# A gate chunk ahead of the attention, selection rounds beside it, and four smaller reorderings in a two-layer decoder trunk

## The chip, the cores and the metric

The kernel runs on one core of a Trainium2 chip. The metric is device time in microseconds of that core, the median of three runs. PE is the matmul engine (its weight loads are PEld), DVE the vector engine, ACT the scalar engine, POOL the GpSimd engine, and SP the engine whose queue issues the weight transfers.

## What is computed

Two layers on 256 tokens of width 1024, all in float32. Each layer mixes tokens by two causal attentions fed by one projection, gates both by sigmoids of that projection, and projects once more; then comes a dense SwiGLU (layer 0) or a top-2-of-8 expert SwiGLU (layer 1), each sub-layer followed by a residual and a LayerNorm.

```python
c_q, c_kv, k_r, dq, dk, dv, iq, ik, iw, gates = split_cols(x @ w_in)
y_a = mla_branch(c_q, c_kv, k_r, pos, ...) @ w_o_mla       # dense causal, 8 heads
y_b = dsa_branch(dq, dk, dv, iq, ik, iw, pos) @ w_o_dsa     # causal, top 64 keys of a query, 8 heads
g = sigmoid(gates); merged = g[..., :D] * y_a + g[..., D:] * y_b
h = merged @ w_out
x = layer_norm(ALPHA * x + h)
f = swiglu(x) if layer 0 else sum over 8 experts of comb[:, e] * swiglu_e(x)
x = layer_norm(ALPHA * x + f)
```

## The kernel before

Each engine has its own program, an order written out by hand, and semaphores between them. All large products are float32 by splitting: a weight unit of 128 x 2048 values (1 MB) lands in one of seven slots (`raw`), ACT casts it to its leading part (`make_head`, `job_head`), DVE subtracts that to get the rest (`make_rest`, `job_rest`), both into one of three slots (`split`), and PE then makes three matmuls for every block of 128 rows (`product`, lines 1528 to 1530): rest of the activations by head of the weights, head by head, head by rest. A head waits until PE has used the unit three before; a rest waits for its head; PE waits for the rest. SP refills a slot of `raw` when its rest is made.

A layer's mixer (`pe_mixer`) projects nine chunks of 512 columns (the last 456), each of two units and two token tiles. Chunks 0 to 4 hold what the attentions need (units 0 to 9). Units 10 to 12 are the latent projections, units 13 and 14 are chunk 5, units 15 to 20 are chunks 6, 7 and 8, all gate columns. Units 21 to 28 are the branch and output projections.

On the first layer PE turns the first half of x (`turn_half`), makes unit 0 for token tile 0, turns the second half of x, makes unit 0 for tile 1, and goes on to unit 1, which needs the second half. ACT and DVE copy every turned half into its head and rest (`cast_x`, `rest_x`).

The attention runs over 16 units (8 heads of the dense kind, then 8 of the sparse kind), software-pipelined on PE: in step i come `qk(i)`, one gate piece, `turn_probs(i - 2)`, in steps 2 to 9 a second gate piece, and `pv(i - 3)`. A gate piece is six matmuls; chunks 6 to 8 have 24. `qk(u)` waits for the row maxima of unit u - 2. DVE makes the maxima (`maxima(u)`); beside them stand the rests of units 17 to 22, five of eight selection rounds (`best_keys`; two max and two replace operations each), `selection`, and `norm_heads(0)`, which waits for `pv(7)` and which `pv(8)` waits for. Two rounds stand ahead of the attention and one much earlier. ACT makes the exponentials (`exps`), copies turned probabilities (`turned_probs`), evacuates gate chunks (`chunk_tile`) and casts heads 17 to 23.

The experts run as eight jobs of 42 units each (`all_jobs`, `JOB`; w1 and w3 in two halves for each of seven hidden groups g, then w2). Of the first job: before its fourth unit DVE has a block of small operations on one partition and on the expert weights, from the wait for `pos_mm` to `routed` (lines 1048 to 1066). In the middle of the job, ACT casts all of x (line 747) and DVE subtracts (line 1131), for the gather of experts 1 and 2 (`gather_pair`), which PE starts at the last w3 of the job. At its end DVE scales x into y (line 1140). POOL makes the picks of the pair (`pair_picks`, line 575) once the expert weights are there.

Of the kernel before, what the change touches and what calls it, by code (L numbers as in the profile page):

```python
# [18 lines left out]
ALU = mybir.AluOpType  # L19
# [6 lines left out]
P = 128  # L26
# [126 lines left out]
def build(nc, a, out):  # L153
    ctx = ExitStack()
    with ctx:
# [328 lines left out]

        def by_slot(b):

            return b[:, :].rearrange("p (k s) -> p k s", k=2)
# [211 lines left out]
        def act_experts(act):  # L699
# [9 lines left out]
            def job(j, kind):  # L709
# [19 lines left out]
                for m, (w, g, half) in enumerate(JOB):  # L729
# [15 lines left out]
                    if kind == "first" and (w, g, half) == ("w2", 2, 0):  # L745
                        act.wait_ge(rests_made, EARLY[0] + 1)
                        act.copy(x_parts[HEAD][:, :, :], x[:, :, :]).then_inc(x_head_made, 1)
# [16 lines left out]
        def _(act):  # L764
# [25 lines left out]
            for l in range(DEPTH):  # L790
# [94 lines left out]
                chunk_tile(ATT, 1)  # L885

# [16 lines left out]
                for i in range(16 + 1):  # L903
# [4 lines left out]
                    if i == 0:  # L908
                        head(17)
                    if i == 2:  # L910
                        head(18)
                    if i in (3, 4):
                        chunk_tile(6, i - 3)
                    if i == 5:
                        head(19)
                    if i == 6:
                        head(20)
                    if i in (7, 8):
                        chunk_tile(7, i - 7)
                    if i == 9:  # L920
                        head(21)
                    if i == 11:
                        head(22)
# [81 lines left out]
        def dve_experts(dve, step):  # L1005
# [42 lines left out]
            E = EXPERTS  # L1048
            dve.wait_ge(pos_mm, 2)
            over, s1, s2, s4 = (flags[0:1, i * 16:(i + 1) * 16] for i in range(4))  # L1050
            step(dve.tensor_scalar(over[:, E:2 * E], bank[4][0:1, 0:E], float(CAP), None, ALU.is_gt))

            dve.wait_ge(exp_done, 1)
            step(dve.tensor_tensor(r_exp, r_exp, r_sel, ALU.mult))
            step(dve.reduce_sum(r_one[:, :, 1:2], r_exp, AX_X))
            step(dve.reciprocal(r_one[:, :, 2:3], r_one[:, :, 1:2]))
            dve.tensor_tensor(r_comb, r_exp, r_one[:, :, 2:3].to_broadcast([P, T, EXPERTS]), ALU.mult).then_inc(placed, 1)
            dve.wait_ge(placed, 1)
            dve.tensor_copy(cur[:, 2:4], r_comb[:, :, 0:1].rearrange("p t n -> p (t n)")).then_inc(comb_put, 1)

            for src, dst, by in ((over, s1, 1), (s1, s2, 2), (s2, s4, 4)):
                step(dve.tensor_tensor(dst[:, E:2 * E], src[:, E:2 * E], src[:, E - by:2 * E - by], ALU.add))
            step(dve.tensor_copy(jobs[0:1, 0:E], over[:, E:2 * E]))
            step(dve.tensor_tensor(jobs[0:1, E:2 * E], s4[:, E:2 * E], over[:, E:2 * E], ALU.subtract))
            step(dve.tensor_copy(jobs[0:1, 2 * E:2 * E + 1], s4[:, 2 * E - 1:2 * E]))
            dve.sem_inc(routed, 1)
# [22 lines left out]
            def job(j, kind):  # L1089
# [28 lines left out]
                for m, (w, g, half) in enumerate(JOB):  # L1118
# [10 lines left out]
                    if kind == "first" and (w, g, half) == ("w2", 2, 1):  # L1129
                        dve.wait_ge(x_head_made, 1)  # L1130
                        dve.tensor_tensor(x_parts[REST][:, :, :], x[:, :, :], x_parts[HEAD][:, :, :].bitcast(F32), ALU.subtract).then_inc(x_rest_made, 1)
# [6 lines left out]
                if kind == "first":  # L1138
                    for t in range(T):
                        step(dve.tensor_scalar(y[:, t, :], x[:, t, :], ALPHA, None, ALU.mult))  # L1140
# [15 lines left out]
        def _(dve):  # L1156
# [133 lines left out]
            for l in range(DEPTH):  # L1290
# [123 lines left out]
                best_keys(range(1, 3))  # L1414
# [23 lines left out]
                for u in range(16):  # L1438
                    maxima(u)
                    if u == 0:  # L1440
                        rest(17)
                    if u < 5:
                        best_keys(range(3 + u, 4 + u))
# [608 lines left out]
```

## Time and profile before

| what | us |
|---|---|
| median of three runs | 1624.46 (1624.42 to 1627.68) |
| the profiled execution | 1625.77 |
| its span, first to last instruction | 1624.1 |
| PE busy | 1591.0 (98%) |
| DVE busy | 1293.2 (80%) |
| ACT busy | 1024.6 (63%) |

The span is what the profile's rows lie in; 1.7 us lie around it. Busy shares are averages over stages. A matmul's own duration is longer than its distance to the next, since they overlap: 512 columns are shown with 390 ns and follow each other every 228 ns. So a wait of PE is read from a gap or from a bracket behind a row, not from the busy share.

### The profile page before, as it was taken

What the parts mean: (1) busy time and instruction counts of PE and PEld (TensorE: products, weight loads), DVE (VectorE), ACT (ScalarE), POOL (GpSimd) and SP (SyncE); (2) the same over time, 40 slices, a digit from 0 to 9 for tenths busy, and PEclk for the clock granted to TensorE, in tenths of its full rate; (3) what the DMA queues carried; (4) which work ended last, traced back from release to release, by engine and by line L of the source; (5) the groups of instructions that cost most, each with busy time, mean ns of one, the idle gap of its engine ahead of it and who ended that gap; (6) DMA issues with size and microseconds to landing.
All of it is one profiled execution on the core that took longest, in us unless ns stands there. A gap on an engine that the chain in (4) does not pass through costs nothing.

```text
span 1624.1 us, 19196 instructions
## 1 busy us (share of the span) xinstructions
PE 1591.0 (98%) x7629; PEld 1322.8 (81%) x7630; DVE 1293.2 (80%) x1302; ACT 1024.6 (63%) x947; POOL 58.9 (4%) x54
## 2 busy tenths in 40 slices
PE   8999999999999999999999999999999999999996
PEld 7888788888788788878888888888888888888885
DVE  6794675445788468899889888889888889888887
ACT  5655544343465645776777776777776777776773
POOL 0000000000000002000000100000100000100000
PEclk9999999999999999999999999999999999999998
DMA  9543366556453355999999999999999999999992
GB/s 326 181 140 117 105 219 208 184 184 201 135 176 130 104 181 178 361 358 324 368 372 363 362 377 328 366 378 365 370 373 327 366 375 360 373 374 328 370 372 85
DMA packets 230687, 453.13 MB, mean 279 GB/s; under 512 B 9920, under 2 KB 15552, under 8 KB 230592
## 3 DMA queue, kind: packets, MB, share of 16 engines
q1 hardware_dynamic: 228400, 447.60, 78.1%
q10 hardware_dynamic: 2192, 4.23, 0.7%
q8 instruction: 63, 1.03, 0.3%
q14 instruction: 32, 0.26, 0.0%
HBM read 450.75 MB, written 1.05 MB: 278 GB/s over the span
## 4 chain that ended last, share of the span: by engine, by line
PE 90%; DVE 7%; ACT 2%; issue 1%; DMA 0%; DVEq 0%; ACTq 0%
PE bank L1528 27%; PE bank L1530 27%; PE bank L1529 27%; PE bank L2003 3%; DVE split L425 2%; PE bank L1698 1%; ACT split L419 1%; PE bank L1916 1%; DVE split L441 1%; PE bank L1889 0%; PE bank L1890 0%; PE bank L1727 0%; PE bank L1726 0%; ACT split L436 0%; DVE x L1241 0%
## 5 line engine op out<-in xcount | busy, mean ns | idle before, releaser
L441 DVE TENSOR_TENSOR split<-raw,split 128x2048 fp32r<-128x2048 f32 x327 | 747.7, 2289 | 103.1 <-ACT split L436 101.9
L436 ACT CAST split<-raw 128x2048 fp32r<-128x2048 f32 x327 | 625.5, 1914 | 185.5 <-PE bank L1530 185.5
L1528 PE MATMUL bank<-split,xe_pair 128*128 128x512 f32 x784 | 310.0, 395 | 0.5 <-DVE split L441 0.5
L1530 PE MATMUL bank<-split,xe_pair 128*128 128x512 f32 x784 | 305.9, 390 | 0.0
L1529 PE MATMUL bank<-split,xe_pair 128*128 128x512 f32 x784 | 305.3, 389 | 0.0
L425 DVE TENSOR_TENSOR split<-raw,split 128x2048 fp32r<-128x2048 f32 (+3 forms) x96 | 208.3, 2174 | 111.3 <-ACT split L419 110.9
L419 ACT CAST split<-raw 128x2048 fp32r<-128x2048 f32 (+3 forms) x96 | 174.4, 1817 | 168.6 <-PE bank L1530 168.3
L1528 PE MATMUL bank<-split,xT 128*128 128x512 f32 (+2 forms) x544 | 217.8, 400 | 4.3 <-DVE split L425 2.4
L1530 PE MATMUL bank<-split,xT 128*128 128x512 f32 (+2 forms) x544 | 208.7, 384 | 0.0
L1529 PE MATMUL bank<-split,xT 128*128 128x512 f32 (+2 forms) x544 | 208.7, 384 | 0.0
L1528 PE MATMUL bank<-split,hT 128*128 128x512 f32 x488 | 190.6, 391 | 0.0
L1530 PE MATMUL bank<-split,hT 128*128 128x512 f32 x488 | 190.0, 389 | 0.0
L1529 PE MATMUL bank<-split,hT 128*128 128x512 f32 x488 | 190.0, 389 | 0.0
L1530 PEld LDWEIGHTS bank<-split,xe_pair 128*128 128x128 f32 x784 | 147.2, 188 | 31.4
L1528 PEld LDWEIGHTS bank<-split,xe_pair 128*128 128x128 f32 x784 | 147.2, 188 | 29.8 <-issue 0.9
L1529 PEld LDWEIGHTS bank<-split,xe_pair 128*128 128x128 f32 x784 | 147.4, 188 | 29.3
L1528 PEld LDWEIGHTS bank<-split,xT 128*128 128x128 f32 x544 | 102.6, 189 | 30.6 <-issue 10.1
L1530 PEld LDWEIGHTS bank<-split,xT 128*128 128x128 f32 x544 | 102.7, 189 | 20.3
L1529 PEld LDWEIGHTS bank<-split,xT 128*128 128x128 f32 x544 | 102.9, 189 | 17.7
L1530 PEld LDWEIGHTS bank<-split,hT 128*128 128x128 f32 x488 | 91.6, 188 | 19.2
L1528 PEld LDWEIGHTS bank<-split,hT 128*128 128x128 f32 x488 | 91.7, 188 | 18.7 <-DVE hT L970 0.2
L1529 PEld LDWEIGHTS bank<-split,hT 128*128 128x128 f32 x488 | 91.6, 188 | 18.5
(248 smaller groups left out, 1604.1 us busy)
## 6 DMA issues: line engine op xcount, KB each, us to landing
raw<-moe_w_dram SPq DMA_DIRECT2D x330, 1024.0 KB, 6.1
raw<-w_in_dram SPq DMA_DIRECT2D x31, 1024.0 KB, 5.1
raw<-dense_w_dram SPq DMA_DIRECT2D x30, 1024.0 KB, 5.1
raw<-w_out_dram SPq DMA_DIRECT2D x8, 1024.0 KB, 5.1
early<-moe_w_dram SPq DMA_DIRECT2D x6, 1024.0 KB, 14.0
raw<-w_o_mla_dram SPq DMA_DIRECT2D x4, 1024.0 KB, 5.1
raw<-w_o_dsa_dram SPq DMA_DIRECT2D x4, 1024.0 KB, 5.4
raw<-w_in_dram SPq DMA_DIRECT2D x4, 912.0 KB, 5.2
```

The lines of the kernel that those rows point to most:

```text
L419: act.copy(split[:, n % SPLIT, HEAD, 0:k * cols], raw[:, n % RAW, 0:k * cols]).then_inc(heads_made, 1)
L425: dve.tensor_tensor(split[:, n % SPLIT, REST, 0:k * cols], raw[:, n % RAW, 0:k * cols], split[:, n % SPLIT, HEAD, 0:k * cols].bitcast(F32) ...
L436: act.copy(split[:, n % SPLIT, HEAD, :], landing(n, j)[:, :]).then_inc(heads_made, 1)
L441: dve.tensor_tensor(split[:, n % SPLIT, REST, :], landing(n, j)[:, :], split[:, n % SPLIT, HEAD, :].bitcast(F32), ALU.subtract).then_inc(r ...
L1528: pe.matmul(out_, act_[REST], w[HEAD], start=first, stop=False)
L1529: pe.matmul(out_, act_[HEAD], w[HEAD], start=False, stop=False)
L1530: return pe.matmul(out_, act_[HEAD], w[REST], start=False, stop=last)
L1698: ins = pe.matmul(bank[4 + u % 2][:, t * P:t * P + keys], q, kk, start=True, stop=True)
L1916: ins = pe.matmul(bank[PAIR_BANKS[r]][:, i * 2 * CAP:(i + 1) * 2 * CAP], x_parts[part][:, t, k * P:(k + 1) * P], pair_pick[:, t, :], start ...
L2003: return pe.transpose(dst, src, ident[:, :])
```

## The change

- On layer 0, PE turns the second half of x after the first two blocks of unit 0, tile 0, where before it did so after all four.
- All eight pieces of chunk 6 go ahead of the attention; in every one of the 16 steps there is one gate piece, of chunk 7 or 8. ACT casts heads 17 and 18 and evacuates chunk 6 ahead of its first exponentials, and the other heads and evacuations follow at new steps.
- On DVE three more selection rounds stand ahead of the attention (five instead of two), with rest 17 between them; rounds 6 and 7 follow in steps 1 and 3, `selection` in step 5, rests 18 to 22 after steps 2, 6, 9, 12 and 14.
- In the first expert job the block of small operations goes behind the rest that follows the fourth unit's `hidden(0)`. The cast and the subtraction of x become four pieces of 512 columns, in the w2 of groups 1 to 4. The scaling into y becomes four pieces beside w3 of groups 3 to 6.

```diff
@@ act, expert jobs
-                    if kind == "first" and (w, g, half) == ("w2", 2, 0):
+                    if kind == "first" and (w, half) == ("w2", 0) and 1 <= g <= 4:
+                        t, at = piece_of_x(g - 1)
                         act.wait_ge(rests_made, EARLY[0] + 1)
-                        act.copy(x_parts[HEAD][:, :, :], x[:, :, :]).then_inc(x_head_made, 1)
+                        act.copy(x_parts[HEAD][:, t, at], x[:, t, at]).then_inc(x_head_made, 1)
@@ act, ahead of and beside the attention
                 chunk_tile(ATT, 1)
+                head(17)
+                for t in range(T):
+                    chunk_tile(6, t)
+                head(18)
...
-                    if i == 0:
-                        head(17)
-                    if i == 2:
-                        head(18)
-                    if i in (3, 4):
-                        chunk_tile(6, i - 3)
-                    if i == 5:
+                    if i == 4:
                         head(19)
-                    if i == 6:
+                    if i in (6, 8):
+                        chunk_tile(7, (i - 6) // 2)
+                    if i == 8:
                         head(20)
-                    if i in (7, 8):
-                        chunk_tile(7, i - 7)
-                    if i == 9:
+                    if i == 10:
                         head(21)
-                    if i == 11:
+                    if i == 12:
                         head(22)
@@ dve, expert jobs
-            (wait for pos_mm, weights, crowding, routed: lines 1048 to 1066)
+            def weights_and_crowding(): (the same lines)
...
-                    if kind == "first" and (w, g, half) == ("w2", 2, 1):
-                        dve.wait_ge(x_head_made, 1)
-                        dve.tensor_tensor(x_parts[REST][:, :, :], x[:, :, :], ...)
+                    if kind == "first" and (w, g, half) == ("w3", 0, 1):
+                        weights_and_crowding()
+                    if kind == "first" and (w, half) == ("w2", 1) and 1 <= g <= 4:
+                        t, at = piece_of_x(g - 1)
+                        dve.wait_ge(x_head_made, g)
+                        dve.tensor_tensor(x_parts[REST][:, t, at], x[:, t, at], ...)
+                    if kind == "first" and (w, half) == ("w3", 0) and g >= NG - 4:
+                        t, at = piece_of_x(g - (NG - 4))
+                        step(dve.tensor_scalar(y[:, t, at], x[:, t, at], ALPHA, None, ALU.mult))
...
-                if kind == "first":
-                    for t in range(T):
-                        step(dve.tensor_scalar(y[:, t, :], x[:, t, :], ALPHA, None, ALU.mult))
@@ dve, ahead of and beside the attention
                 rest(16)
-                best_keys(range(1, 3))
+                best_keys(range(1, 4))
+                rest(17)
+                best_keys(range(4, 6))
...
-                    if u == 0:
-                        rest(17)
-                    if u < 5:
-                        best_keys(range(3 + u, 4 + u))
-                    if u == 4:
+                    if u == 2:
                         rest(18)
+                    if u in (1, 3):
+                        best_keys(range(6 + u // 2, 7 + u // 2))
+                    if u == 5:
+                        selection()
                     if u == 6:
-                        selection()
-                    if u == 7:
                         rest(19)
-                    if u == 8:
+                    if u == 9:
                         rest(20)
                     if u == 10:
                         norm_heads(0)
-                    if u == 11:
+                    if u == 12:
                         rest(21)
-                    if u == 13:
+                    if u == 14:
                         rest(22)
@@ pe_mixer
                     if (l, c, half) == (0, 0, 0) and i % 2 == 0:
+                        if (i, t) == (2, 0):
+                            pe.wait_ge(x_in2, 16)
+                            for tile in range(T):
+                                turn_half(0, tile, 1)
                         pe.wait_ge(rests_made if i else first_rest, 1)
...
+            for f in range(8):
+                gate_piece(f)
...
-            f = 0
+            f = 8
...
-                if 2 <= i < 10:
-                    gate_piece(f)
-                    f += 1
@@ gather_pair
-                    pe.wait_ge(x_rest_made, 1)
+                    pe.wait_ge(x_rest_made, 2 * T)
```

## Rows read from the trace of the kernel before

**Rows 1.** The page, section 1: busy time, share of the span, instructions.

```profile
PE 1591.0 (98%) x7629; PEld 1322.8 (81%) x7630; DVE 1293.2 (80%) x1302; ACT 1024.6 (63%) x947; POOL 58.9 (4%) x54
```

**Rows 2.** Who PE waited for: us in total, times, longest.

```profile
PE bank L1698 <- DVE mx L1428: 3.8, 2, 1.9
PE bank L1528 <- DVE split L441: 2.8, 3, 1.2
PE bank L1528 <- DVE split L425: 2.4, 2, 2.2
```

**Rows 3.** Timeline of the start: start, duration, engine, line, operation, idle before.

```profile
10.39 0.40 PE L1530 MATMUL bank<-split,xT 128*128 128x512 f32 x1
...
12.28 1.03 PE L2003 MATMUL bank<-ident,x 128*128 128x128 f32 x8
...
12.91 1.08 ACT L777 CAST xT<-bank 128x512 fp32r<-128x512 f32 x2 [3.74 <-PE bank L2003]
...
15.83 4.49 DVE L425 TENSOR_TENSOR split<-raw,split 128x2048 fp32r<-128x2048 f32 x2 [1.00 <-ACT split L419]
...
18.26 0.71 PE L1528 MATMUL bank<-split,xT 128*128 128x512 f32 x1 [2.18 <-DVE split L425]
```

**Rows 4.** The tile x in the first 20 us: second load's issue; times to landing.

```profile
L506 SPq DMA_DIRECT2D x<-x_dram x1: 470/470/470, 2.3 to 2.3; - x1
...
DMA to landing us min/median/max: 4.1/5.6/7.0
```

**Rows 5.** Stretches: PE, PEld, DVE, ACT, POOL busy; granted clock; DMA share, GB/s.

```profile
18.00:22.00 4.00, 3.74 (x10) 2.96 (x11) 3.83 (x11) 1.81 (x1) 0.00 (x0) 0.57 1.03 380
108.00:113.00 5.00, 3.10 (x15) 2.29 (x15) 4.80 (x22) 1.35 (x5) 0.00 (x0) 1.00 0.58 201
168.00:172.00 4.00, 4.00 (x12) 3.11 (x11) 3.45 (x4) 2.27 (x5) 0.00 (x0) 0.57 0.02 4
```

**Rows 6.** Timeline at the entry of the attention, layer 0.

```profile
104.58 1.89 ACT L419 CAST split<-raw 128x2048 fp32r<-128x2048 f32 x1
...
106.50 2.29 DVE L425 TENSOR_TENSOR split<-raw,split 128x2048 fp32r<-128x2048 f32 x1 [2.85 <-ACT split L419]
...
108.71 0.61 DVE L1343 MAX8 top<-score 128x8 f32<-128x128 f32 x2
...
110.14 0.29 DVE L1425 CUSTOM_DVE_ANT_0 sm<-bank,causal 128x128 f32<-128x128 f32 x1
...
111.04 0.92 PE L1698 MATMUL bank<-kTm,qTm 96*128 96x128 f32 x4 [1.90 <-DVE mx L1428]
```

**Rows 7.** Timeline: starts of qk(6), qk(7); of qk(10), qk(11).

```profile
124.35 0.87 PE L1698 MATMUL bank<-kTm,qTm 96*128 96x128 f32 x4
...
128.78 0.87 PE L1698 MATMUL bank<-kTm,qTm 96*128 96x128 f32 x4
...
142.54 0.92 PE L1698 MATMUL bank<-dT 64*128 64x128 f32 x4
...
145.78 0.92 PE L1698 MATMUL bank<-dT 64*128 64x128 f32 x4
```

**Rows 8.** Timeline of DVE: norm_heads(0) begins, and what follows it.

```profile
145.88 0.20 DVE L1434 RECIPROCAL rden<-den 128x8 f32<-128x8 f32 x1 [1.54 <-PE bank L1727]
...
147.56 0.28 DVE L1425 CUSTOM_DVE_ANT_0 sm<-bank,select 128x128 f32<-128x128 f32 x1
```

**Rows 9.** Timeline at the start of the first expert job.

```profile
637.56 0.15 DVE L1051 TENSOR_SCALAR flags<-bank 1x8 f32<-1x8 f32 x1
...
639.09 5.97 POOL L575 TENSOR_SCALAR pair_pick<-slot_no,small 128x128 fp32r<-128x128 f32 x3 [0.22 <-POOL small L570]
...
640.17 4.49 DVE L441 TENSOR_TENSOR split<-raw,split 128x2048 fp32r<-128x2048 f32 x2 [0.34 <-DVE jobs L1065]
...
642.52 0.50 PE L1528 MATMUL bank<-split,xeT 128*128 128x512 f32 x1 [1.23 <-DVE split L441]
```

**Rows 10.** Timeline: x into its rest, and the scaling into y.

```profile
701.36 2.29 DVE L1131 TENSOR_TENSOR x_rest_part<-x,x_head 128x2048 fp32r<-128x2048 f32 x1
...
754.57 1.41 DVE L1140 TENSOR_SCALAR y<-x 128x1024 f32<-128x1024 f32 x2
```

More of the change, by code:

```diff
@@ L483, in pair_half, with piece_of_x @@
             return slice(CAP, 2 * CAP) if kind == "even" else slice(0, CAP)
+        def piece_of_x(i):
+            return i // 2, slice(i % 2 * W, (i % 2 + 1) * W)
         def by_slot(b):
@@ L1046, in dve_experts @@
             make_rest(dve, FIRST + SPLIT - 1)
[L1048 to L1063, printed above, removed]
@@ L1064, in dve_experts, with weights_and_crowding @@
-            step(dve.tensor_tensor(jobs[0:1, E:2 * E], s4[:, E:2 * E], over[:, E:2 * E], ALU.subtract))
-            step(dve.tensor_copy(jobs[0:1, 2 * E:2 * E + 1], s4[:, 2 * E - 1:2 * E]))
-            dve.sem_inc(routed, 1)
+            def weights_and_crowding():
+                E = EXPERTS
+                dve.wait_ge(pos_mm, 2)
+                over, s1, s2, s4 = (flags[0:1, i * 16:(i + 1) * 16] for i in range(4))
+                step(dve.tensor_scalar(over[:, E:2 * E], bank[4][0:1, 0:E], float(CAP), None, ALU.is_gt))
+                dve.wait_ge(exp_done, 1)
+                step(dve.tensor_tensor(r_exp, r_exp, r_sel, ALU.mult))
+                step(dve.reduce_sum(r_one[:, :, 1:2], r_exp, AX_X))
+                step(dve.reciprocal(r_one[:, :, 2:3], r_one[:, :, 1:2]))
+                dve.tensor_tensor(r_comb, r_exp, r_one[:, :, 2:3].to_broadcast([P, T, EXPERTS]), ALU.mult).then_inc(placed, 1)
+                dve.wait_ge(placed, 1)
+                dve.tensor_copy(cur[:, 2:4], r_comb[:, :, 0:1].rearrange("p t n -> p (t n)")).then_inc(comb_put, 1)
+                for src, dst, by in ((over, s1, 1), (s1, s2, 2), (s2, s4, 4)):
+                    step(dve.tensor_tensor(dst[:, E:2 * E], src[:, E:2 * E], src[:, E - by:2 * E - by], ALU.add))
+                step(dve.tensor_copy(jobs[0:1, 0:E], over[:, E:2 * E]))
+                step(dve.tensor_tensor(jobs[0:1, E:2 * E], s4[:, E:2 * E], over[:, E:2 * E], ALU.subtract))
+                step(dve.tensor_copy(jobs[0:1, 2 * E:2 * E + 1], s4[:, 2 * E - 1:2 * E]))
+                dve.sem_inc(routed, 1)
@@ L1128, in job @@
                         turned(g - 1)
-                    if kind == "first" and (w, g, half) == ("w2", 2, 1):
-                        dve.wait_ge(x_head_made, 1)
-                        dve.tensor_tensor(x_parts[REST][:, :, :], x[:, :, :], x_parts[HEAD][:, :, :].bitcast(F32), ALU.subtract).then_inc(x_rest_made, 1)
+                    if kind == "first" and (w, g, half) == ("w3", 0, 1):
[3 more added lines that the diff above has]
+                        dve.wait_ge(x_head_made, g)
+                        dve.tensor_tensor(x_parts[REST][:, t, at], x[:, t, at], x_parts[HEAD][:, t, at].bitcast(F32), ALU.subtract).then_inc(x_rest_made, 1)
+                    if kind == "first" and (w, half) == ("w3", 0) and g >= NG - 4:
+                        t, at = piece_of_x(g - (NG - 4))
+                        step(dve.tensor_scalar(y[:, t, at], x[:, t, at], ALPHA, None, ALU.mult))
                     if kind in PAIR_GATHER and (w, g, half) == ("w3", NG - 1, 1):
@@ L1606, in pe_mixer @@
                     if (l, m) == (0, 0):
-                        keep_warm(pe, t, 0 if t else 4)
-                        pe.wait_ge(x_in2 if t else x_in, 16)
-                        for tile in range(T):
-                            turn_half(0, tile, t)
-                        keep_warm(pe, t, 0 if t else 4)
+                        if t == 0:
+                            keep_warm(pe, 0, 4)
+                            pe.wait_ge(x_in, 16)
+                            for tile in range(T):
+                                turn_half(0, tile, 0)
+                            keep_warm(pe, 0, 4)
                     if m == 0:
```

## Prediction

> **What bounds the kernel now.** First the busy shares: PE is busy for 98% of the span [rows 1]. Matmuls that merely follow one another cannot be made fewer by a reordering, and this change neither adds nor removes one. So all it can win is time in which PE stands still or runs slowly, and I read that directly: the table of who PE waited for. It has three lines that the change touches [rows 2]: the first qk that waits for a row maximum, 3.8 us in two times, one in each layer; rests of expert units, 2.8 us in three times; rests of mixer units, 2.4 us in two times, of which 2.2 us is one wait. That is 9.0 us out of 1624. The third view is the granted clock. After the 2.2 us wait at the start PE runs at 1.2 GHz for a while: the mean clock of 18 to 22 us is 0.57, so 4 x 0.43 = 1.7 us are lost there besides the wait. The same happens after the end of the attention, 168 to 172 us, and nothing of that kind after the wait at the entry of the attention, clock 1.00 in 108 to 113 us [rows 5]. Weight transfers are no bound in the rows of waits: no expert unit of PE, nor its head or rest, waits for a landing. If PE gets faster by some microseconds, the queues in front of it are filled by rests that are themselves released by PE, so they move with it.
>
> **The start (layer 0 only).** Before, PE turned the second half of x at 12.28, ACT began its casts at 12.91, and DVE could begin rest 1 at 15.83, after waiting 1.00 us for the head; PE went on at 18.26 [rows 3]. After, the turn comes behind six matmuls of unit 0 whose last begins at 10.39 and takes 0.23: at 10.62. The second half of x was issued at 2.3 and landed 7.0 us later, at 9.3 [rows 4], so the turn does not wait. The whole chain turn, cast, head 1, rest 1, PE moves by 12.28 - 10.62 = 1.66 us. It could be held up by the landing of unit 1, queued right behind x: if 1 MB takes the 2.7 us that a unit of PE lasts, it lands at 12.1, just ahead of the new time at which ACT is free (11.25 + 1.08 = 12.3). I take **1.6 us**, bounds 0.8 and 1.7. PE's own work of unit 0 is unchanged, it only ends 0.3 earlier, at 15.6, so the wait left is about 1.1 us instead of 2.2. On the clock: with 2.2 us of standing still it fell; after 1.9 us at 111.04 and 1.23 us at 642.52 it did not [rows 5, 6, 9]. 1.1 us is below both, so I take the drop as gone: **1.7 us**, bounds 0 and 1.7.
>
> The Trainium skill, page "TensorE: Matmul & The Clock Gate", section "What's actually happening", says that throttled is the default, that activity releases the throttle, and that the moment is run-variable because the monitor runs freely. By this rule a shorter stop is no promise: the drop could stay, or another stop could get one. The sum would then be 1.7 us smaller. The trace agrees with the variable part: a wait of 1.9 us had no drop, and a shorter one at the end of the attention had.
>
> **The attention, its entry (each layer).** Before: head 17 was cast at 104.58 (1.89), rest 17 followed at 106.50, a selection round took 108.71 to 110.14, and only then came the maxima of unit 1, for which PE stood until 111.04 [rows 6]. After, PE has chunk 6 first: 8 pieces x 6 matmuls x 0.228 = 10.9 us, so qk(0) comes at 112.1 instead of 101.2. Its units 15 and 16 are split already at that time (their rests end at about 100.0). DVE in the meantime: three rounds of 1.43, rest 17 of 2.21, two rounds [rows 6] = 9.4 us from 99.9, free at 109.3, ahead of qk(0). The first maxima are then made as soon as qk ends. On ACT head 18 stands behind the evacuation of chunk 6 at 112.1 and ends at about 114.6; a table load and the first exponentials end by about 117, turn_probs(0) is due at 118.2. So the wait of 1.9 us, with the restart 2.1 us from the last matmul, goes.
>
> **The attention, its steps.** A step with two pieces lasts 128.78 - 124.35 = 4.43 us, one with a single piece 145.78 - 142.54 = 3.24 us (456 columns, sparse unit) [rows 7]. Eight pieces leave the steps and eight are added ahead: PE's own work is conserved to within 0.1 us a piece, at nothing in my sum. What is lost is cover. Now every chain has to fit in 3.1 to 3.2 us a step from the first step on. I walked the three queues with the durations above. Maxima take 0.9 from their start [rows 6], a cast of a head 1.9, small ACT copies 0.5 each (1.08 for two [rows 3]), norm_heads 147.56 - 145.88 = 1.7 [rows 8]. The steps 10 to 15 have the same pieces as before, with the same two queues beside them, and had no PE wait, so the steady pitch holds. The one place where the new order is late is pv(8). Head 20 moves from step 6 to step 8. It now stands behind turned_probs(7) and an evacuation: turn_probs(7) begins at 139.1, then 0.5 + 0.4 + 0.5 + 1.8 = head done at 142.3. DVE has rest 20 queued in front of maxima(10) and norm_heads(0): 142.3 + 2.2 + 0.8 + 1.7 = 146.9. PE reaches pv(8) at 145.8 (two steps and 0.2 later). **PE waits about 0.9 us** (0.9 to 1.1 by the walk); bounds 0, if head 20 slips in earlier, and 2, if ACT is a copy later. Behind the waiting pv(8) on PE stands the rest of the attention, so this is paid in full. Net of the attention: 2.1 - 0.9 = 1.2 a layer, **2.4 us** for both. With no new wait 4.2, with 2.0 in each layer 0.2.
>
> **The small operations of the first job.** Before, they took DVE from 637.56 to 640.17, 2.6 us, right in front of rest 3, and PE waited 1.23 us (1.4 with the restart) for it at 642.52 [rows 9]. After, rest 3 begins when its head is done, 637.9, and PE goes on at 641.1. But the 2.6 us come back behind rest 6. A rest can't be far ahead, since its head waits for PE to use the unit three before: DVE ends rest 6 at about 648.2, then 2.6 us, then rest 7 of 2.2: 653.0. PE wants unit 7 at 641.1 + 4 x 2.72 + 0.4 (a turn) = 652.4. It waits 0.6, and 0.1 more for the next DVE step. **Gain 0.7 us**, bounds 0 and 1.4.
>
> These operations also release POOL's picks, whose first three took 5.97 us while two rests beside them took 4.49 [rows 9]. The Trainium skill, page "SBUF — State Buffer", section "Who interferes with whom", says that DVE and GpSimd share one pair of ports as an exclusive lock, and that the later one blocks fully. By that rule the picks would now fall on rests 7 to 9, which have no slack, and the 0.7 us could be gone; by the rows, two rests beside the picks lasted as long as two without them [rows 3], and the sum keeps it.
>
> **x in four pieces.** The subtraction of x, 2.29 us of DVE at 701.36 [rows 10], caused the second of the three expert waits, 1.06 us, with a follow-up of 0.1 to 0.2. A fourth of it is 0.6 us; DVE is idle 2.5 us of the 16.8 us of a group, and in w2 of each group a rest begins over 1 us ahead of its due time. ACT's pieces are 0.5 instead of 1.9. gather_pair now waits for four pieces, the last made in group 4, a whole group ahead. **Gain 1.2 us**, bounds 0.8 and 1.2.
>
> **y in four pieces.** 1.41 us of DVE at 754.57 [rows 10] made the third wait, the remaining 0.5 of the 2.8 [rows 2]. Pieces of 0.4 in groups 3 to 6, hidden by the same 2.5 us; groups 3 and 4 then have 1.0 us of both. **Gain 0.5 us**, bounds 0 and 0.6.
>
> **Sum.** 1.6 + 1.7 + 2.4 + 0.7 + 1.2 + 0.5 = 8.1 us. The profiled execution took 1625.77 (span 1624.1, the rest around it), so it would take 1617.7. The median of the runs is 1.3 us below the profiled one; I take the difference off the median: 1624.46 - 8.1 = **1616.4 us**.
>
> **The rivals.** (a) *The clock drop stays*, or moves to another stop: all waits go as said, 1.7 us less won, 1618.1. For it: the drop at the end of the attention follows shorter stops than the one now at the start. Against it: the stop is halved. (b) *The softmax chain is late in more places.* Each layer pays 1 to 2 us more, at the first turn_probs (1.2 us of slack in the walk), or in the expert job the 0.7 goes: 1618.5 to 1621. (c) *Better than said*: no wait at pv(8), or one clock drop at the end of an attention goes as well: 1613.0 to 1614.7. (d) *The change does not do what it says*: the time comes back at the next wait at each place, as at pv(8), 1624. (e) *Slower*: with one piece a step, the chain maxima, exponentials, copy sets the pitch, not PE, in the steps 0 to 9 where rounds and selection are added to it. Then these steps stay near the old 4.43 us while the 10.9 us of chunk 6 are paid ahead: 8 x 1.3 x 2 = 20.8 us lost, 8.1 + 1.7 won at most, about 1636. It decides against the change as soon as the steps of one layer lose 4.1 us to waits. Against it: steps 10 to 15 ran at 3.24 with up to 2.3 us of DVE and 1.9 us of ACT work added in a step, and a round is only 1.43.
>
> **Chances.** Forecast within 1.2 us: 0.50. (a) 0.20, (b) 0.12, (c) 0.08, (d) 0.05, (e) 0.05. The measurement can tell 0.2%, 3.2 us, from no change: faster means below 1621.2. Forecast, (a), (b) and (c) lie there: 0.90; (d) is the same, 0.05; (e) slower, 0.05. The range goes from the middle of (c), 1614.0, to the upper part of (b), 1620.2, and leaves out a little under 2 in 10.
>
> **What would show it.** Start: PE goes on to unit 1 at about 16.6, and 16 to 22 us have clock 1.00. Entry: no wait of L1698 for maxima; qk(0) near 108.8 (112.1 less the 3.3 won at the start). One new wait in each layer, pv(8) (L1725) for DVE's normed heads, near 0.9 us. First job: no wait at unit 3, one of about 0.6 at unit 7, none at x and y. Wrong would be: several waits for maxima or probabilities, a low clock at the start, or a rest in the first job late by more than 1 us.

## The result, and the profile after

| what | before | after |
|---|---|---|
| median | 1625.18 (4 runs, 1624.42 to 1627.68) | 1616.04 (4 runs, 1615.95 to 1618.1) |
| ratio | | 0.9944, 95% interval 0.9927 to 0.9961 |
| the profiled execution | 1625.77 | 1618.1 |
| its span | 1624.1 | 1616.3 |

9.1 us less (6.3 to 11.9 by the interval); forecast were 1616.4 and, as a sum, 8.1 us off a median of 1624.46, which with a fourth run is 1625.18. The changed kernel's profiled execution is the slowest of its four; the other three lie within 0.15 us of each other.

The changed kernel's page, section 1 (busy time, share, instructions) and the engines' shares of the chain that ended last:

```profile
PE 1589.0 (98%) x7629; PEld 1322.7 (82%) x7630; DVE 1293.8 (80%) x1307; ACT 1025.6 (63%) x950; POOL 57.0 (4%) x54
...
PE 95%; DVE 3%; ACT 1%; issue 1%; DMA 0%; DVEq 0%; ACTq 0%
```

The busy time is that of [rows 1] to within 2 us, with the same 7629 matmuls. What changed is who PE waited for, and there the answer to [rows 2] is (total us, times, longest):

```profile
PE bank L1739 <- ACT pT L910: 1.7, 2, 0.9
...
PE bank L1739 <- DVE proj L1444: 1.6, 2, 0.8
...
PE bank L1535 <- DVE split L425: 1.0, 2, 0.8
PE bank L1535 <- DVE split L441: 0.7, 1, 0.7
```

The line of the maxima (3.8 us) is gone. L441, the rests of expert units, went from 2.8 to 0.7 and from three waits to one; L425, the rests of mixer units, from 2.4 to 1.0. One line is new, L1444: pv(8) waits for the normed heads, 0.8 us in each layer. The first line was there before, with the same 1.7 us.

The early turn of x (first row) and the three places where PE now waits, from the timeline of PE, to be read beside [rows 3], [rows 8] and [rows 9]:

```profile
11.23 1.03 PE L2014 MATMUL bank<-ident,x 128*128 128x128 f32 x8
...
17.22 0.47 PE L1535 MATMUL bank<-split,xT 128*128 128x512 f32 x1 [0.82 <-DVE split L425]
...
144.30 0.41 PE L1739 MATMUL bank<-proj,pT 128*128 128x64 f32 x2 [0.81 <-DVE proj L1444]
...
648.42 0.50 PE L1535 MATMUL bank<-split,xeT 128*128 128x512 f32 x1 [0.67 <-DVE split L441]
```

The granted clock after the start stop, answering the first of [rows 5], and at the ends of the two attentions (busy time of PE, PEld, DVE, ACT, POOL; clock; DMA share; GB/s):

```profile
18.00:22.00 4.00, 4.00 (x19) 3.33 (x18) 3.72 (x12) 1.64 (x1) 0.00 (x0) 1.00 1.03 379
...
160.00:168.00 8.00, 6.17 (x28) 4.91 (x28) 5.09 (x7) 6.34 (x9) 0.00 (x0) 0.79 0.01 2
556.00:566.00 10.00, 8.17 (x50) 7.03 (x49) 4.87 (x7) 8.80 (x16) 0.00 (x0) 0.87 0.26 100
```

The low clock behind the start stop is gone (0.57 before); both ends of the attention still have theirs.

**Stretches.** To see where time went, every trace is divided at the same PE instructions, and the columns are the distances between their starts: the first product of unit 0 and the first product of unit 1; qk(0); the first branch matmul (oT); the first matmul on the dense hidden values (hT); the same for layer 1; the first unit of the first expert job; the first of the second job; the last PE instruction. The table is worked out from the timelines of PE. "Low" counts the places before the second job where eight or so large matmuls follow each other every 0.43 us instead of 0.228, that is at 1.2 instead of 2.4 GHz; a full one costs 1.5 to 1.7 us. A short one is one to four such matmuls at the very start. "Start overfill" is the first, mis-sized version of "start filled".

```
kernel     unit0-unit1  -qk(0)  -oT    -hT    -qk(0)  -oT    -job1  -job2   -end    low
before            9.12   82.90  66.56  89.11  244.23  66.56  65.22  125.61  853.48  3
after             8.05   92.19  54.39  89.12  255.15  54.38  65.23  123.35  853.17  2 + a short one
turn only         8.34   81.33  68.18  89.13  244.38  66.57  65.25  125.57  853.26  3 + a short one
attention only    9.13   93.81  54.37  87.57  255.27  54.39  63.69  125.61  853.32  1
experts only     10.82   82.91  66.52  89.11  244.27  66.56  65.22  123.34  853.20  4
start filled      9.05   81.35  68.18  89.11  244.26  66.59  65.22  125.61  853.39  3
start overfill   12.59   81.33  66.55  87.56  244.26  68.15  65.21  125.61  853.37  3
ends filled       7.44   92.22  54.33  87.60  255.26  54.34  63.71  123.31  853.22  0
head 20 early     7.45   92.20  53.32  89.06  255.14  53.32  63.68  123.34  853.22  1
rounds beside     7.79   92.20  54.37  89.10  255.26  54.38  65.21  123.35  853.27  2 + a short one
block alone       9.12   82.90  66.54  87.58  244.38  68.17  65.24  125.38  853.42  3
block in six      7.99   92.22  54.38  89.09  255.14  54.37  65.25  122.25  853.21  2 + a short one
three at once     7.43   92.22  53.28  88.63  255.12  53.28  63.70  122.26  853.25  1 shorter, in the LayerNorm
```

The same stretch has the same length in every kernel that has the same order in it, to within 0.15 us (0.3 in the long last one), or it differs by about 1.6 us: a low stretch that one execution has and another has not. So a part of the change is read by subtracting lengths, and the clock is read apart from it. What the table leaves out is the 12.1 us behind the last matmul. They are the same in every profile but that of the attention part alone, where they are 14.3, since DVE stood still there with nothing that it waited for; in the kernel before it waited 0.57 us at that place:

```profile
1611.84 0.21 DVE L1226 BATCH_NORM_AGGREGATE mv<-stat 128x2 f32<-128x12 f32 x1 [2.73 <-issue]
```

So not every difference between two executions is the clock's. For the executions without a trace there is the mean granted clock of each. It is 0.997 in the profile without a low stretch, 0.996 or 0.995 in those with one or two, and 0.994 or 0.993 in those with three or four: an estimate from these is 0.001 for each.

### The profile page after: what moved, and what is told of

It reads as the page before. It is cut to its first block, busy times and chain, and to the rows that moved or that the text cites. A ratio compares the mean times of both kernels' runs of the same rounds, so it can differ in the third digit from the quotient of the medians.

```text
span 1616.3 us, 19203 instructions
## 1 busy us (share of the span) xinstructions
PE 1589.0 (98%) x7629; PEld 1322.7 (82%) x7630; DVE 1293.8 (80%) x1307; ACT 1025.6 (63%) x950; POOL 57.0 (4%) x54
## 4 chain that ended last, share of the span: by engine, by line
PE 95%; DVE 3%; ACT 1%; issue 1%; DMA 0%; DVEq 0%; ACTq 0%
PE bank L1535 29%; PE bank L1537 29%; PE bank L1536 29%; PE bank L2014 4%; PE bank L1712 1%; PE bank L1927 1%; ACT split L419 1%; PE bank L1900 0%; PE bank L1901 0%; DVE split L441 0%; DVE x L1248 0%; PE bank L1741 0%; PE bank L1740 0%; PE bank L1739 0%; DVE xT L973 0%
## 5 line engine op out<-in xcount | busy, mean ns | idle before, releaser
L441 DVE TENSOR_TENSOR split<-raw,split 128x2048 fp32r<-128x2048 f32 x327 | 747.8, 2290 | 100.4 <-ACT split L436 99.6
L425 DVE TENSOR_TENSOR split<-raw,split 128x2048 fp32r<-128x2048 f32 (+3 forms) x96 | 208.2, 2175 | 111.2 <-ACT split L419 110.8
## 6 DMA issues: line engine op xcount, KB each, us to landing
early<-moe_w_dram SPq DMA_DIRECT2D x6, 1024.0 KB, 14.3
```

The lines of the kernel that those rows point to most:

```text
L425: dve.tensor_tensor(split[:, n % SPLIT, REST, 0:k * cols], raw[:, n % RAW, 0:k * cols], split[:, n % SPLIT, HEAD, 0:k * cols].bitcast(F32) ...
L441: dve.tensor_tensor(split[:, n % SPLIT, REST, :], landing(n, j)[:, :], split[:, n % SPLIT, HEAD, :].bitcast(F32), ALU.subtract).then_inc(r ...
```

## The experiments

### Do the parts add up?

Three kernels, each with one part of the change in the kernel before. First the early turn of x alone:

```diff
                     if (l, c, half) == (0, 0, 0) and i % 2 == 0:
+                        if (i, t) == (2, 0):
+                            pe.wait_ge(x_in2, 16)
+                            for tile in range(T):
+                                turn_half(0, tile, 1)
```

> The kernel before with only the second turn of x moved up in unit 0. My theory: the stop ahead of unit 1 shrinks from 2.2 us to about 1 us (gain 1.0 to 1.6, depending on how late the first loads land) and no low clock follows it (gain 1.7): 2.7 to 3.3 us below before, 1621.2 to 1622. Rival, the low clock comes by chance and not from the stop: 1.0 to 1.6 us only, and a stretch at 1.2 GHz still somewhere in 16 to 22 us.

1624.46, ratio 0.9982 (0.9973 to 0.9992) to the kernel before, 1627.0 in that session: 2.9 us by the ratio, 2.5 by the medians, where 2.7 to 3.3 were expected. But the trace says more. In the first two stretches it wins 0.78 (1.68 less 0.9 for the first four matmuls of unit 0, from 9.14 us, which ran at half rate right behind the very first stop) and 1.57 (the low stretch at 18.8 us), and then it has one that the kernel before had not, at the entry of the attention:

```profile
109.00:112.00 3.00, 3.00 (x13) 2.36 (x13) 2.86 (x16) 2.02 (x9) 0.00 (x0) 0.68 0.63 243
```

Then the attention part alone (chunk 6 ahead, the new order of heads, rests, rounds and evacuations):

> The kernel before with only the attention's part (chunk 6 and rounds ahead, one piece a step). My theory: the wait of qk for maxima (1.9 us) goes in both layers, a wait of pv(8) for normed heads of 0.8 to 0.9 us comes: 2.4 us below before. Rival, the time comes back in other steps of the attention: within 0.5 us of before. Rival, the clock after the attention moves with it: up to 1.7 us more or less a layer.

1622.27, ratio 0.9978 (0.9966 to 0.9989), 3.6 us by the ratio, 4.7 by the medians. From unit 1 to the first branch matmul it is 93.81 + 54.37 = 148.18 against 149.46, so 1.28 us in the first layer, and 255.27 + 54.39 against 244.23 + 66.56, 1.13, in the second: 2.4 us as expected. Its profile has two low stretches fewer than that of before, and its eleven executions have a mean clock of 0.9951 where the 35 of the kernel before in that session have 0.9935. So this part gains clock too, by the estimate above one to two low stretches, and that fits the rest of the median. The turn alone has 0.9940, too little above 0.9935 to tell.

The expert part alone:

> The kernel before with only the three moves in the first expert job. My theory: waits of 1.23, 1.06 and 0.47 us go, one of 0.6 to 0.7 at unit 7 comes: 2.4 us below before. Rival, POOL's picks beside rests 7 to 9 hold DVE up: the wait at unit 7 is 1.4 us or more and the gain at most 1.7 us.

1624.91, ratio 0.9983 (0.9972 to 0.9994), 2.8 us by the ratio, 2.1 by the medians; its first job is 2.27 us shorter. What follows is 0.28 shorter, of which only the 0.12 of the next unit is the change's: that stretch is also 0.22 shorter with the early turn alone. Together 2.4 us, as expected, and with a wait of 0.68 at unit 7 the rival is out. The three gains are 2.9 + 3.6 + 2.8 = 9.3 us against 9.1 for the change, but each of them is uncertain by 1.5 to 1.9 us, so this sum proves little. The stretches say it better: with the low ones taken off, the first job (123.34 and 123.35) and layer 1's attention (309.66 and 309.53) are as long in the part alone as in the whole change. The waits of one part do not depend on another; of the clock that is not shown.

### What is the clock worth, and can it be held?

The start stop filled with small matmuls in the kernel before, without moving anything. A call of `keep_warm` multiplies the identity by itself, 128 columns, into a bank that nobody reads then. A first version had 36 of them, which was mis-sized: they took 4.18 us in a stop of 2.2, and it came to 1627.29, ratio 1.0002 (0.9992 to 1.0013), where 1.7 us less had been expected. This one has 18:

```diff
+                    if (l, m, t) == (0, 1, 0):
+                        keep_warm(pe, 5, 9)
                     chunk(m // 2, m % 2, t)
```

> The kernel before with 9 calls of a small float32 matmul on a free bank in the stop ahead of unit 1. In p2_warm_stop the 18 calls had become 36 matmuls of 0.11 us, 4.0 us in a stop of 2.3, so the clock's price was hidden by the overfill; 9 calls are 18 matmuls, 2.0 us. Stop causes the drop: full clock in 18 to 22 us, from the first matmul of unit 1 to qk(0) 81.3 us as in p1 and p2 (before: 82.9), about 1.6 us below before in the median. Rival, the drop there comes by chance: 82.9 us in that segment and a time equal to before.

```profile
15.82 2.17 PE L2000 MATMUL bank<-ident 128*128 128x128 f32 x18
...
18.10 0.50 PE L1528 MATMUL bank<-split,xT 128*128 128x512 f32 x1
...
18.00:22.00 4.00, 3.90 (x17) 3.25 (x18) 3.83 (x11) 1.90 (x1) 0.00 (x0) 1.00 1.05 385
...
109.00:113.00 4.00, 3.65 (x14) 2.96 (x14) 3.79 (x21) 2.34 (x9) 0.00 (x0) 0.66 0.63 246
```

The clock behind the start is 1.00 and that stretch 1.55 us shorter. Yet the median is 1625.46 against 1625.56, ratio 0.9999 (0.999 to 1.0008). In the profiled execution the low stretch had moved on: 0.66 in 109 to 113 us, behind the entry stop, where the kernel before has 1.00 in 108 to 113 [rows 5]. The kernel with the early turn alone had it there too. In the six kernels with the old entry, a low stretch follows 4 of the 12 entry stops: two in layer 0, in these two kernels, which have none behind the start stop, and two in layer 1. The overfilled kernel speaks against the simple reading: it has none behind the start stop either, and none at the entry of layer 0, but one at the entry of layer 1. Yet whichever stops have one, five of these six profiles count three and the sixth four. That a low clock taken away at one stop is taken up by a later one is what this suggests, on few executions; that filling one stop alone wins nothing in the median is measured, and my expectation was a miss.

Then all stops at the end of the attention of the changed kernel filled, 3 calls ahead of the last pv and 4 ahead of the first branch:

```diff
+                if i == 18:
+                    pe.wait_ge(row_max, 16 * (l + 1))
+                    keep_warm(pe, 4, 3)
                 if i >= 3:
                     pv(i - 3)
...
+            keep_warm(pe, 4, 4)
             pe.wait_ge(o_rest, 4 * l + 2)
             branch_tile("oa", 0, 0, 0)
```

> The changed kernel with 6 small matmuls in the stop ahead of pv(15) and 8 in the stop ahead of the first branch product (0.7 and 0.9 us in stops of 0.86 and 0.97), in both layers. If the low clock after the attention follows from these stops: clock 1.00 in 163 to 168 and 562 to 567 us, 3.1 us below the changed kernel where that had both drops, less than that in the median, since not every execution has them. Rival, the drop comes from the thin work of the last steps (small matmuls), which stays: drops as before and the same time.

```profile
160.00:168.00 8.00, 7.81 (x45) 6.55 (x44) 5.09 (x7) 5.65 (x9) 0.00 (x0) 1.00 0.01 3
556.00:566.00 10.00, 9.81 (x60) 8.32 (x60) 5.09 (x7) 6.85 (x10) 0.00 (x0) 1.00 0.19 55
```

1614.43 (1614.13 to 1615.61), ratio 0.9937 (0.9923 to 0.995): 1.6 us below the changed kernel's 1616.04 where up to 3.1 were expected; that one was measured in another session, with intervals that overlap. PE reaches the branches at the same distance (54.33 against 54.39), but both stretches behind it are 1.5 us shorter (87.60 and 63.71), and there is no low stretch up to the second job. In this execution the low clock did not move on: the start stop is short, the entry has none, and both ends are filled. Over all the profiles, 17 of the 22 ends that are not filled have a low stretch, and none of the four that are filled, these two and two in the last kernel below. But that last kernel has one in the LayerNorm instead, and two of the five executions here have a mean clock of 0.996. And the kernel with head 20 early (below), measured in the same session with nothing filled, has a mean clock of 0.9968 against 0.9966 here. That filling removes the low stretch behind the filled stop is shown; how much of it the median keeps is not.

### Which order on ACT and DVE matters in the attention?

Head 20 one step earlier in the changed kernel, since pv(8) waits behind it:

```diff
-                    if i == 8:
+                    if i == 7:
                         head(20)
```

> The changed kernel with ACT's cast of head 20 one step earlier (step 7 instead of 8). My theory of the one new wait: pv(8) waits for norm_heads(0), which stands behind rest 20, which waits for head 20. Then rest 20 is made a step earlier, the wait of 0.8 us of pv(8) goes in both layers, and the kernel is 1.6 us below the changed one (hT0 of layer 0 to the first branch matmul of layer 1: 308.7 instead of 309.5 us). Rival, norm_heads(0) is late for another reason (it also waits for pv(7)): the wait stays 0.8 us. Rival, the exponentials of step 8 are late instead: a new wait of turn_probs.

ACT and DVE ahead of pv(8), first in the changed kernel, then with head 20 early:

```profile
137.91 1.73 ACT L419 CAST split<-raw 128x1824 fp32r<-128x1824 f32 x1
...
139.68 2.06 DVE L425 TENSOR_TENSOR split<-raw,split 128x1824 fp32r<-128x1824 f32 x1 [3.55 <-ACT split L419]
...
142.63 0.69 DVE L1444 TENSOR_TENSOR proj<-bank,rden 128x512 f32<-128x512 f32 x1
```

```profile
135.32 2.05 DVE L425 TENSOR_TENSOR split<-raw,split 128x1824 fp32r<-128x1824 f32 x1
...
140.43 0.69 DVE L1444 TENSOR_TENSOR proj<-bank,rden 128x512 f32<-128x512 f32 x1
...
142.62 0.33 PE L1739 MATMUL bank<-proj,pT 128*128 128x64 f32 x2
```

In the first, DVE sat idle 3.55 us for that head and then had rest 20, the maxima and the norm to do while PE waited. In the second all that is done when pv(8) comes, and the bracket is gone. The stretch is 1.07 us shorter in each layer (53.32), where 0.8 was expected, the length of the bracket. pv(8) itself comes 0.97 us sooner, and its matmuls then start 0.17 us apart instead of 0.24. 1612.93 (1612.74 to 1613.92), ratio 0.9926 (0.9912 to 0.9939): 3.1 below the changed kernel's median of another session, of which 2.1 is this; one low stretch fewer in its profile fits the rest.

The other way: are the rounds ahead of the attention needed, or is chunk 6 enough?

```diff
-                best_keys(range(1, 4))
+                best_keys(range(1, 3))
                 rest(17)
-                best_keys(range(4, 6))
...
-                    if u in (1, 3):
-                        best_keys(range(6 + u // 2, 7 + u // 2))
+                    if u < 5:
+                        best_keys(range(3 + u, 4 + u))
```

> The changed kernel, but only two selection rounds and rest 17 stand ahead of the attention and rounds 3 to 7 stand in steps 0 to 4, one each. Theory 1, the chunk ahead is what removes the entry wait and the place of the rounds is worth nothing: maxima and one round are 2.3 us in a step of 3.04, with rest 18 in step 2 the five steps hold 13.5 of 15.2 us, so no new wait, and the time is within 0.5 us of the changed kernel's. Theory 2, the rounds must leave the steps: step 2 holds 0.85 + 1.43 + 2.2 = 4.5 us of DVE, a qk or a turn_probs waits 1 to 2 us in each layer, and the time is 2 to 4 us above the changed kernel's, 1618 to 1620.

```profile
110.73 0.61 DVE L1350 MAX8 top<-score 128x8 f32<-128x128 f32 x2
...
115.11 2.28 DVE L425 TENSOR_TENSOR split<-raw,split 128x2048 fp32r<-128x2048 f32 x1
...
121.68 0.61 DVE L1350 MAX8 top<-score 128x8 f32<-128x128 f32 x2
```

Five rounds and rest 18 stand between the maxima, and the attention is as long as in the changed kernel: 54.37 and 54.38. Theory 1 holds in the trace. The median is 1617.66 (1614.43 to 1618.32), ratio 0.994 (0.9925 to 0.9955) where the changed kernel had 0.9944. It is 1.6 above the changed kernel's of another session, more than the 0.5 that theory 1 allowed, with runs on both sides of it; but no stretch of the attention or behind it is longer by more than 0.11 us. What removed the entry wait is chunk 6 in front of it, which gives ACT and DVE 10.9 us to get ahead, together with head 17 and rest 17, which stay ahead here too; the two were not tried apart. The place of the rounds is free.

### The small operations of the first expert job

That block alone, moved as in the change, in the kernel before:

> The kernel before with the block of small operations alone moved behind the rest of the fourth unit's hidden half. By the prediction's step: no wait at unit 3 of the first job (1.23 us before), one of 0.6 to 0.7 at unit 7 instead, the waits of the x and y steps unchanged; the first job is 0.7 us shorter than before (125.61 from its first unit to the second job's), 124.9. Rival: the picks on GpSimd, which now fall beside rests 7 to 9, make these rests longer than 2.2 us and the job is no shorter.

```profile
650.51 5.78 POOL L579 TENSOR_SCALAR pair_pick<-slot_no,small 128x128 fp32r<-128x128 f32 x3 [0.22 <-POOL small L574]
...
651.41 4.50 DVE L441 TENSOR_TENSOR split<-raw,split 128x2048 fp32r<-128x2048 f32 x2
...
653.75 0.50 PE L1535 MATMUL bank<-split,xeT 128*128 128x512 f32 x1 [0.64 <-DVE split L441]
```

There is one execution, 1625.73, so only its trace is read. The wait is at unit 7 and 0.64, as said, and two rests beside the picks take 4.50 us, as two without picks do (4.49 [rows 3]): the rival is out. But the job is only 0.23 us shorter, not 0.7. The distances from one unit's start to the next say why: unit 3 comes 1.40 us sooner after its predecessor, unit 7 0.80 later, and units 5, 8 and 9 another 0.17, 0.14 and 0.09. I had priced one late unit; a DVE that has no slack is late for its neighbours too.

Cut into six parts, each behind another rest, in the changed kernel:

```diff
+                    if kind == "first" and m in (1, 3, 6, 9, 12, 15):
+                        small_part((1, 3, 6, 9, 12, 15).index(m))
```

> The changed kernel with the block of small operations of the first expert job cut into six parts of 0.2 to 0.6 us, behind the rests of units 4, 6, 9, 12, 15 and 18 of the job. My theory: the wait at unit 7 (0.67 us) comes only from 2.6 us of DVE in one piece; it goes, first job 0.7 us shorter (122.6 instead of 123.35). Rival, POOL's picks, which these operations release, hold the rests up: the wait stays or moves to where the picks now run.

The wait for L441 is gone and the job 122.25 instead of 123.35: 1.1 us, where 0.7 was expected. With the 0.2 of the move it is 1.3 of the 1.4 us by which unit 3 had been late. The median does not show it, 1616.8 (1614.61 to 1616.99), ratio 0.9945 (0.9931 to 0.9959): such a gain is below what the clock gives and takes from one execution to the next, and only the stretch resolves it.

### The three together

> The changed kernel with three edits at once: head 20 cast one step earlier, the block of small operations cut into six parts behind six rests, small matmuls in the stops at the end of the attention. If the three are independent, against the changed kernel: 1.1 us a layer for head 20 (2.2), 1.1 us in the first job, 1.6 us for a low-clock stretch that does not come: 4.9 us, so about 1611.1 beside the changed kernel's 1616.0; the segments are 53.3 from qk(0) to the first branch matmul in both layers, 87.6 for the branches, 122.2 for the first job. If a part of the gain is only shifted (the wait of 0.9 us for the probabilities that follows pv(8), or a low-clock stretch that moves to another stop, as at the attention's entry when the start was filled), it is nearer 1613.

1612.09 (1611.14 to 1612.34), ratio 0.9909 (0.9893 to 0.9924): 13.5 us below the kernel before, 3.95 below the changed one, and below each of the three single edits, all of other sessions. The stretches are the expected ones, 53.28, 53.28 and 122.26, so the waits that the edits remove are independent. The 1 us by which 1611.1 is missed in the profiled execution stands in one place:

```profile
200.00:225.00 25.00, 23.05 (x143) 20.80 (x142) 17.52 (x26) 10.19 (x12) 1.54 (x2) 0.93 0.46 170
```

a clock of 0.93 around the wait for the LayerNorm: fifteen matmuls of 256 columns behind it ran at half rate, where in the kernel with the ends filled none did (88.63 against 87.60 us). The low clock had moved on after all, to a shorter stretch. Two of the five runs, 1611.14 and 1611.26, are 1 us faster than the other three, with a mean clock of 0.997 instead of 0.995 or 0.996; that they are the ones without it is likely, but they have no trace.

## Why the prediction came out right, step by step

**What bounds it** held: the busy time stayed, the waits went.

**The start gap**, 1.6 us: with no low stretch in it the first stretch is 7.44 instead of 9.12, 1.68 us. In the changed kernel's own profile only 1.07, since its first three matmuls ran at half rate, 0.6 us that I had not thought of. The stop left was forecast as 1.1 us; the row shows 0.82 and the restart. PE went on at 17.22 instead of 16.6, and at 16.5 in the three executions of the same start that have no low stretch there.

**The clock drop**, 1.7 us: right in its place and doubtful as a gain. With the stop shortened or filled, nine profiles of nine have no low stretch behind it; with the stop of 2.2 us, four of four have one, and it costs 1.6. But filling the stop alone won nothing in the median. My step took the drop as a property of its stop, while rival (a) had it move to another, and in the kernels that change the start alone it mostly did. The change does gain clock: 9.1 us in the medians less the 6.6 of the other terms below is 2.5, uncertain by the 2.8 of the interval, and the mean clock of its four executions is 0.9958 where the kernel before has 0.9935 in the session of the parts. But by the same clocks it is mainly the attention part that gains it, 0.0016 of the 0.0023, and the turn 0.0005. So the 1.7 us came out by another route than the step says, and that is luck. Why removing the entry wait saves low stretches, and also those at the ends of the attention, of which that part's profile has none, is open.

**The attention**, 2.4 us: 1.28 (layer 0, in the attention part alone) and 1.26 (layer 1) measured with the clock left out (the latter counted from hT, 310.79 to 309.53), 2.5. The entry wait is gone, pv(8) waits 0.81 where 0.9 was said, and costs 1.07, since with it removed too a layer wins 2.3 where 2.1 was said for the entry; two errors of 0.2 cancel. Its place was right, and the chain head 20, rest 20, maxima, norm is the one in the rows above. qk(0) came at 109.41, forecast "near 108.8", the 0.6 being the start's. I had kept the rounds ahead as part of this; they carry nothing of it.

**The steps**, rival (e): they run at 121.87 - 118.83 = 3.04 us, below the 3.1 to 3.2 that was said, and no qk waits:

```profile
118.83 0.87 PE L1712 MATMUL bank<-kTm,qTm 96*128 96x128 f32 x4
...
121.87 0.87 PE L1712 MATMUL bank<-kTm,qTm 96*128 96x128 f32 x4
```

**The small operations**, 0.7 us: 0.2 (0.23 alone, 0.20 in the changed kernel, at the units ahead of the x pieces). The wait at unit 7 was right (0.67 against 0.6), the small delays of its neighbours were missing. By the Trainium skill, page "SBUF — State Buffer", section "Who interferes with whom", DVE and GpSimd exclude each other on a shared pair of ports, and for that I had feared for the rests. The trace agrees, but on the other side: the pick that begins after a rest has begun takes until both rests are over, and the rests keep their 4.49. In the changed kernel, on POOL and on DVE:

```profile
646.35 4.61 POOL L579 TENSOR_SCALAR pair_pick<-slot_no,small 128x128 fp32r<-128x128 f32 x1
...
650.94 0.60 POOL L579 TENSOR_SCALAR pair_pick<-slot_no,small 128x128 fp32r<-128x128 f32 x1
```

```profile
646.07 4.49 DVE L441 TENSOR_TENSOR split<-raw,split 128x2048 fp32r<-128x2048 f32 x2
...
651.09 2.36 DVE L441 TENSOR_TENSOR split<-early,split 128x2048 fp32r<-128x2048 f32 x1
```

A pick alone takes 0.60; this one ends at 650.96, behind the rests' 650.56. Nobody waits for it then. The last row is the other side: a rest that begins while a pick runs takes 2.36 instead of 2.29. And a pick does not always have to wait for two rests: with the block in six, one at 652.79 took 2.75, one rest long, and the rest right behind took 2.38.

**x and y**, 1.2 and 0.5 us: from the unit starts of the kernel with the expert part alone, the units behind the subtraction of x come 4.05 - 2.83, 2.87 - 2.72 and 2.78 - 2.72 us apart less, 1.43; those behind y 3.35 - 2.72 and 2.84 - 2.72, 0.75. Both were too small for the same reason: I read the bracket and not the units after it.

**The sum.** 1.68 + 1.6 + 2.54 + 0.2 + 1.43 + 0.75 = 8.2 us by the traces, against 8.1 forecast. The errors in the first job (0.5 too much, 0.48 too little) cancel, which is luck again. The profiled executions differ by 1625.77 - 1618.1 = 7.7, which is the 8.2 less the 0.6 at the start. The medians differ by 9.1; three executions of the changed kernel were 2.0 us faster than the profiled one. Their mean clock was 0.996 against 0.995, which fits about one low stretch fewer, but they have no trace, so this stays open. Nor is it known what decides which stops of an execution get one: over the traces here it is none to four.

## What to carry to other kernels

A wait that opens a stage is best removed by putting independent work of the bound engine ahead of it: the 10.9 us of chunk 6 emptied the queues of two other engines, and the place of the rounds in these queues then did not matter; that of head 20, which a later step waits for, did. Price a delayed item by the starts of all units behind it, not by the one bracket. And a gain of 1 to 2 us in a kernel with a switching clock is read from stretches between fixed instructions, while medians decide only on what is larger.

## What was new about the hardware

- After stops of 0.85 and 0.98 us with 0.9 us of small matmuls between them (end of attention) PE ran eight matmuls at half rate in the changed kernel; after one of 1.9 us at the entry it did not in the kernel before, and did in 4 of the 12 entries of its kind. The length of one stop alone doesn't say. The rows of PE at the end of the changed kernel's attention:

```profile
161.94 0.43 PE L1739 MATMUL bank<-proj,pT 128*128 128x64 f32 x2 [0.85 <-ACT pT L910]
...
163.80 0.53 PE L1535 MATMUL bank<-split,oT 128*128 128x512 f32 x1 [0.98 <-issue]
164.13 0.63 PE L1536 MATMUL bank<-split,oT 128*128 128x512 f32 x1
164.55 0.63 PE L1537 MATMUL bank<-split,oT 128*128 128x512 f32 x1
...
167.52 0.40 PE L1535 MATMUL bank<-split,oT 128*128 128x512 f32 x1
```

  Starts 0.42 us apart are 1.2 GHz, 0.23 apart 2.4. The Trainium skill, page "TensorE: Matmul & The Clock Gate", section "What's actually happening", calls the throttled level the default and its moment run-variable. With the second the traces agree: kernels that share most of their order have none to four such stretches.
- Filling stops with matmuls on the identity, of which each call is issued as two (18 in 2.17 us, 0.12 each), won 1.5 us at each end of the attention in the profile, with 0.85 and 0.98 us of stop filled; at the start it won the same in its stretch and nothing in the median.
- Where picks on GpSimd and rests on DVE overlapped, the one that came later paid: a pick up to 4 us, a rest 0.07 to 0.09 us (the rows at the small operations above).
